# Latent attention: transposes and values one unit later, four sets of probabilities, and the exponential issued before the copy

## What is computed

```python
def probs(qb, kk):
    s = jnp.einsum("bqhd,bkhd->bhqk", qb, kk).astype(jnp.float32) * scale
    return jax.nn.softmax(s, axis=-1)
...
q_a = (_rms(acq, lp["mla_q_norm_g"]) @ lp["mla_w_q_up"]).reshape(B, N, H_A, NOPE_A + ROPE_A)
kv = (ckv_all @ lp["mla_w_kv_up"]).reshape(B, T, H_A, NOPE_A + V_A)
k_a = jnp.concatenate([kv[..., :NOPE_A],
                       jnp.broadcast_to(kr_all[:, :, None, :], (B, T, H_A, ROPE_A))], axis=-1)
o_a = _attend(jnp.concatenate([q_nope, q_rope], axis=-1), k_a, kv[..., NOPE_A:]).reshape(B, N, H_A * V_A)
```

## Time and profile before

| | us |
|---|---|
| median of 3 runs | 2758.0 |
| least and most of the runs | 2754.29, 2760.59 |
| the profiled execution | 2755.17 |
| its span, first to last instruction | 2753.3 |
| TensorE busy | 2599.3 (94% of the span) |
| GpSimd busy | 1329.9 (48%) |
| VectorE busy | 1184.5 (43%) |
| ScalarE busy | 742.3 (27%) |
| chain that ended last | PE 85%, DVE 8%, ACT 2% |

### The profile page before, as it was taken

How to read it: one execution, slowest core, us unless ns; L and a number is a source line. 1 busy time by engine, 2 the same in 40 slices (tenths; PEclk the granted TensorE clock), 3 DMA queues, 4 the chain that set the end, 5 groups by cost and what they waited for, 6 DMA issues and landing times.

```text
span 2753.3 us, 41706 instructions
## 1 busy us (share of the span) xinstructions
PE 2599.3 (94%) x17328; PEld 2405.0 (87%) x17328; DVE 1184.5 (43%) x1708; ACT 742.3 (27%) x1332; POOL 1329.9 (48%) x604
## 2 busy tenths in 40 slices
PE   4999989999999999999979999898999999999997
PEld 3879986777999899999968799668789998999997
DVE  4434255777224522232554422658752173132233
ACT  2252235215312312021123313351343023021121
POOL 2534540340565566666645255205226665666663
PEclk8999999999999999999999899999999999999999
DMA  6201215430222122222211022242102221222221
GB/s 249 69 16 60 68 58 183 170 129 1 71 75 70 62 77 74 73 77 77 74 57 47 17 74 71 93 169 85 39 27 74 77 70 62 77 70 76 77 75 56
DMA packets 62555, 215.33 MB, mean 78 GB/s; under 512 B 6688, under 2 KB 11168, under 8 KB 62112
## 3 DMA queue, kind: packets, MB, share of 16 engines
q1 hardware_dynamic: 56448, 203.97, 21.8%
q10 hardware_dynamic: 5920, 8.70, 0.9%
HBM read 208.15 MB, written 4.49 MB: 77 GB/s over the span
## 4 chain that ended last, share of the span: by engine, by line
PE 85%; DVE 8%; ACT 2%; DVEq 2%; issue 1%; DMA 1%; ACTq 1%; SPq 1%
PE big L459 22%; PE big L462 22%; PE big L463 22%; PE big L614 4%; PE last_two L645 2%; PE two L628 2%; PE last_two L541 1%; PE big L482 1%; DVE cols L1356 1%; PE two L759 1%; PE big L485 1%; PE big L486 1%; PE last_two L759 1%; DMA first_mod<-in_first 1%; DVE sq L1701 1%
## 5 line engine op out<-in xcount | busy, mean ns | idle before, releaser
L427 POOL TENSOR_TENSOR w_hi<-raw,cst 128x1024 fp32r<-128x1024 f32 x288 | 556.8, 1933 | 1295.4 <-PE big L459 1183.4
L459 PE MATMUL big<-act_hi,w_hi 128*128 128x320 f32 x2784 | 871.0, 313 | 21.6 <-ACT stage L1208 6.5
L462 PE MATMUL big<-act_lo,w_hi 128*128 128x320 f32 x2784 | 864.4, 310 | 0.0
L463 PE MATMUL big<-act_hi,w_lo 128*128 128x320 f32 x2784 | 864.1, 310 | 0.0
L430 POOL TENSOR_TENSOR w_lo<-raw,w_hi 128x1024 fp32r<-128x1024 f32 x288 | 742.4, 2578 | 41.0
L459 PEld LDWEIGHTS big<-act_hi,w_hi 128*128 128x128 f32 x2784 | 526.7, 189 | 32.5 <-issue 29.4
L462 PEld LDWEIGHTS big<-act_lo,w_hi 128*128 128x128 f32 x2784 | 526.9, 189 | 0.9
L463 PEld LDWEIGHTS big<-act_hi,w_lo 128*128 128x128 f32 x2784 | 526.3, 189 | 0.0
L459 PE MATMUL big<-u_hi,w_hi 128*128 128x320 f32 (+1 forms) x1024 | 320.6, 313 | 12.7 <-DVE cols L1793 10.8
L462 PE MATMUL big<-u_lo,w_hi 128*128 128x320 f32 (+1 forms) x1024 | 319.2, 312 | 0.0
L463 PE MATMUL big<-u_hi,w_lo 128*128 128x320 f32 (+1 forms) x1024 | 318.8, 311 | 0.0
(11 more groups left out here) (301 smaller groups left out, 3504.3 us busy)
## 6 DMA issues: line engine op xcount, KB each, us to landing
raw<-in_w SPq DMA_DIRECT2D x368, 512.0 KB, 3.5
first_mod<-in_first SPq DMA_DIRECT2D x16, 512.0 KB, 15.7
x<-in_x ACTq DMA_DIRECT2D x1, 2560.0 KB, 12.6
out_y<-x SPq DMA_DIRECT2D x8, 320.0 KB, 2.3
cst<-in_const ACTq DMA_DIRECT2D x1, 1664.0 KB, 10.9
small<-in_small ACTq DMA_DIRECT2D x2, 437.0 KB, 8.9
out_C<-c_new ACTq DMA_DIRECT2D x2, 258.0 KB
v_d<-in_past ACTq DMA_DIRECT2D x2, 256.0 KB, 3.0
```

The lines of the kernel that those rows point to most:

```text
L427: nc.gpsimd.tensor_tensor(w_hi[:, to, :], raw[:, slot, :], ones[:, 0:1].to_broadcast([P, BLK]), ALU.mult)
L459: first = mm(ps, wh, ah, start=k == 0, stop=False)
L462: mm(ps, wh, al, start=False, stop=False)
L463: last = mm(ps, wl, ah, start=False, stop=k == nk - 1)
```

## The change

The lag of transposes and values becomes a number per kind of attention: 2 for the latent attention (it was 1), 1 for the differential attention as before. In the latent attention:

- TensorE issues turn(i-2) instead of turn(i-1), and the values of the pair that ends with unit i-3.
- There are four sets of probabilities: two in `prob_a`, and `t1` and `rs` as one set each. The columns of maxima and sums go round four places instead of two, in both attentions.
- ScalarE issues exps(i+1) first and copyT(i-2) behind it. In the differential attention the exponentials stood first before and still do.
- The `w_mod` blocks stand in steps 5 to 8, the row's copy in step 9, its transposes and the keeping in step 10, one step later each.
- VectorE's outputs come one step later.

The diff, without its lines on waits that only count anew:

```diff
+MLA_LAG, DIFF_LAG = 2, 1
+COPY_FIRST = {1: False, 2: False}
...
-        neg_max, row_sum = cols[:, 12:16], cols[:, 16:20]
+        neg_max, row_sum = cols[:, 12:20], cols[:, 20:28]
...
+        LAG = {1: MLA_LAG, 2: DIFF_LAG}
+
         def prob_tile(prob, maps, i, m):
 
-            return prob[:, maps * (i % 3) + m, :] if i % 3 < 2 else (t1, rs)[m]
+            n = i % (LAG[maps] + 2)
+            if n < 2:
+                return prob[:, maps * n + m, :]
+            if maps == 1:
+                return (t1, rs)[n - 2]
+            return (t1, rs)[m] if n == 2 else sq[:, m, :]
...
-                    if p < 4 and 4 <= at < 8:
-                        if at == 4:
+                    if p < 4 and 5 <= at < 9:
+                        if at == 5:
...
-                        for k in (2 * at - 8, 2 * at - 7):
+                        for k in (2 * at - 10, 2 * at - 9):
                             mod_block(l, KD * q + k, one[1][:, 256:512])
-                    if p < 4 and at == 9:
-                        mod_turn(l, q, one[1][:, 256:512])
+                    if i >= 10 and at == 0:
+                        mod_turn(l, q - 1, one[1][:, 256:512])
...
-                for i in range(-1, n + 2):
+                lag = LAG[maps]
+                for i in range(-1, n + lag + 1):
                     if i + 1 < n:
                         scores(i + 1)
                     if beside and 0 <= i:
                         beside(i)
-                    if 0 <= i - 1 < n:
-                        turn(i - 1)
-                    if 0 <= i - 2 and (i - 2) % side == side - 1:
-                        if beside and i % 10 == 1:
-                            pe.wait_ge(mod_kept, l * MOD_CHUNKS + 3 + (i - 11) // 10)
-                        values((i - 2) // side)
+                    if 0 <= i - lag < n:
+                        turn(i - lag)
+                    j = i - lag - 1
+                    if 0 <= j and j % side == side - 1:
+                        if beside and j % 10 == 9:
+                            pe.wait_ge(mod_kept, l * MOD_CHUNKS + 3 + j // 10)
+                        values(j // side)
...
                 def exps(i):
                     h, t = units[i]
-                    if i >= 3:
-                        act.wait_ge(pT_ready, l * 60 + unit0 + i - 2)
+                    lag = LAG[maps]
+                    if i >= lag + 2:
+                        act.wait_ge(pT_ready, l * 60 + unit0 + i - lag - 1)
...
-                for i in range(-1, n + 1):
-                    if i >= 1 and maps == 1:
-                        copyT(i - 1)
+                lag = LAG[maps]
+                for i in range(-1, n + lag):
+                    if i >= lag and COPY_FIRST[maps]:
+                        copyT(i - lag)
                     if i + 1 < n:
                         exps(i + 1)
-                    if i >= 1 and maps == 2:
-                        copyT(i - 1)
+                    if i >= lag and not COPY_FIRST[maps]:
+                        copyT(i - lag)
...
-                    if i % 10 == 8:
+                    if i % 10 == 9 and i < 40:
                         keep_row(l, 2 + i // 10, one[1][:, 256:512])
```

More of the change, by code:

```diff
@@ L960, in exps @@
                         ps, b, _ = buf(use)
-                        col = 2 * (i % 2) + m
+                        col = 2 * (i % 4) + m
                         act.wait_ge(maxed, l * 80 + exp0 + maps * i + m + 1)
@@ L1361, in normalise @@
                     n = CTX if t == LATE else T
-                    c0 = 2 * (i % 2)
+                    c0 = 2 * (i % 4)
                     dve.wait_ge(exped, l * 80 + exp0 + maps * (i + 1))
@@ L1385, in attend @@
                 n = len(units)
-                for i in range(-1, n + 3):
+                lag = LAG[maps]
+                for i in range(-1, n + lag + 2):
                     if i + 1 < n:
@@ L1393, in attend @@
                         normalise(i)
-                    if i >= side + 2 and i % side == 0:
-                        outputs((i - side - 2) // side)
+                    j = i - lag - 2
+                    if j >= 0 and j % side == side - 1:
+                        outputs(j // side)
                     if beside and i >= 0:
@@ L1445, in hook @@
                 def hook(i):
-                    if i % 10 == 9 and i < 40:
-                        q = 2 + i // 10
+                    if i % 10 == 0 and 10 <= i <= 40:
+                        q = 1 + i // 10
                         keep_mod(l, q, q, one[1][:, 256:512])
```

## The result

The changed kernel takes 2781.7 us (median of 5 runs, 2777.3 to 2787.7) against 2758.0: the ratio is 1.0088, with a 95% interval of 1.0069 to 1.0107. The forecast was 2778, slower, with a range of 2765 to 2787.

What follows compares the result with a forecast made beforehand. TensorE's work plus its waits bounds the kernel. Adding +17 us for the chain and +3 for the blocks' loads to the 2758.0 us median gave 2778 us, range 2765 to 2787 (8 in 10).

Steps and rivals of the forecast that it cites:

- What bounds: Whole kernel: TensorE's work plus its waits, busy 94% of the span; the change touches only the two latent attention stages.
- the sign: Latent attention in the profile after: both stages last 116 to 119 us each, with TensorE still busy about 102.
- The chain: Latent attention: scores' start through maximum, exponential and copy to next step's turn takes about 4.0 us; TensorE's cover is 3.0 to 4.2.
- The period: Ten units of latent attention take 29.0 us against 26.5; waits of 1.3, 1.1, 0.3, 0.7 in steps 10, 12, 13, 14.
- The sum: Both latent attention stages: 7.5 us from three periods plus 1 outside them, 8.5 per layer, +17 us for two.
- The loads: Fourth block pair of each period has less time for its loads: 0.5 us on average in 8 periods, +3 us.
- The clock: Latent attention: new waits are no longer than today's 1.7 us, so the granted clock keeps 2.4 GHz.
- rival C: TensorE falls to 1.2 GHz in parts of the stage, 10 us in each of 8 periods: 2858 us; chance 2%.
- A: Faster: copies behind the early exponential are always in time, 4.8 us of waits per layer vanish: 2748 us; chance 5%.
- B: Nothing measurable: the new waits shrink to what they replace, 2753 to 2763 us; chance 5%.
- E: Slower by half: only the waits of steps 10 and 12 arise, 2.4 against 1.1 us: 2768 us; chance 15%.
- D: Slower with the loads: every fourth block pair waits a full microsecond or two: 2785 us; chance 15%.

Runs made afterwards that it cites:

- the grid: Eight versions combining lag 1 or 2, exponential or copy first, old or later block and row steps; ratios to the kernel before from 1 to 1.0088.
- the version with the lowest ratio: Against the kernel before: lag 2, copy first, blocks spread over steps 5 to 9, row's transposes in step 11, row kept before outputs; 2753.5 us, ratio 0.9977.

## Why the prediction was right

- **What bounds.** Right: the two stages grew by 24.4 us of the 26.7 between the two profiled executions, and most of what came in were waits of TensorE. The stages last 119.5 and 121.9 us, more than the 116 to 119 that I gave as the sign.
- **The chain.** Right in every link. Start of scores 12 to maximum 1.38 (forecast 1.38), to the exponential 0.92 (0.86 taken), to the copy 1.06 (1.00), to the transposes 0.42 (0.42 for the short copy). That a ready copy is held behind a waiting exponential is what the grid shows: with the exponential first there are 8.0 to 12.3 us of copy waits per layer in all four cells, with the copy first 0 to 3.5.
- **The period.** Forecast 29.0, measured 29.7, with waits of 1.42, 1.24, 0.26 and 0.78 (forecast 1.3, 1.1, 0.3 and 0.7) at the places forecast; 0.4 of the 0.7 us that are missing is the pair of blocks that a load split. Transposes of the probabilities no longer wait for VectorE, as forecast.
- **The sum: two terms, both short.** Forecast +17 for the chain and +3 for the loads, measured +24.4. The part of the loads can be taken out: from the start of a pair of blocks to the next instruction, idle time ahead of the pair included, the sixteen pairs of a layer took 16.0 and 17.2 us before and take 18.2 and 20.5 now. So the loads cost 5.5 us, and about 19 are left for the chain. The chain's waits in the period above are 3.7 us instead of 3.4: I took 0.86 for maximum to exponential, where it is 0.92, and an interval of the differential attention for exponential to copy, where it is 1.06 instead of 1.00. That is 0.3 us in each of six whole periods, 1.8 in all, and fills the gap between 17 and 19.
- **The loads.** Forecast +3, measured +5.5; this is the larger part of what was missing. TensorE's named waits for the ring account for 3.5 of it (1.0 and 3.4 us, where layer 1 had 0.9 before). The other 2 are what a pair loses beyond its idle time when a load splits it, which I hadn't priced. Per period the loads cost 0.8 us, where I took 0.5 from a span of 0 to 1.
- **The clock.** 1.00 in both stages of the profiled execution, as forecast, but this was in part luck: seven of the twelve kernels below show a fall of the clock in one stage or both, behind waits no longer than 1.7 us. A fall costs about 2 us there, not the 10 for each period that rival C priced.
- **Rivals.** A fell: the change removed the waits for probabilities and still lost; it would have needed the chain under 3.0 us. And the version nearest to A, copy first at lag 2, isn't faster either, so my price for A (-10 us) was wrong by itself: waits that are taken away come back at the next thing in line (the row, the loads, VectorE's outputs). B and E fell by the stages. D took 10 us for the loads; the 5.5 lie between it and my own 3.

My expectations for the experiments were worse than the prediction, and mostly too hopeful (only the later steps alone turned out cheaper than I expected): of the six versions from which I expected some microseconds off the kernel before, two show it beyond their interval, by 4 us at most.

## What to carry to other kernels

On an in-order engine, an instruction that waits for new work must not stand ahead of one that is ready and that somebody waits for: with a single buffer behind it (here the one tile of transposes), the whole chain from new scores to the old copy falls on the engine that bounds. A deeper pipeline didn't help here: the lag of 2 lost 4 to 10 us in the four pairs of the grid, in two of them clear of the noise. Whether a second tile for the transposes would have changed that wasn't tried. Lay the chain from start to start against the work that covers it, step by step, and look for the steps that lack their cover; and when waits are taken away, ask what is second in line before the gain is booked.

One place is left where this could be put to use. The differential attention has its exponentials first in every version, and TensorE waits for its copies in the kernel before (layer 0, 606 to 720 us):

```profile
PE two L628 <- ACT probT_d L978: 2.2, 5, 0.5
```

No run put the copy first there, so what that is worth isn't known.

## What the runs showed that I had not expected

**The clock falls in this stage in some executions.** In layer 0 of the version with copy first and old steps, TensorE waited 1.00 and 0.60 us for two loads:

```profile
426.43 0.64 PE L550 MATMUL last_two<-raw,cond 128*32 128x256 f32 x8 [1.00 <-DMA raw<-in_w]
...
427.67 0.64 PE L550 MATMUL last_two<-raw,cond 128*32 128x256 f32 x8 [0.60 <-DMA raw<-in_w]
...
431.54 2.40 PE L654 MATMUL last_two<-probT_a,v_a 128*64 128x128 f32 x20
...
437.78 1.31 PE L654 MATMUL last_two<-probT_a,v_a 128*64 128x128 f32 x20
```

The values at 431.54 last 2.40 us, the same 20 matmuls at 437.78 last 1.31. The stretches view gives the clock:

```profile
425.00:430.00 5.00, 3.25 (x27) 1.87 (x25) 1.02 (x4) 0.82 (x3) 0.00 (x0) 0.84 0.76 267
430.00:436.00 6.00, 5.69 (x32) 4.46 (x33) 0.70 (x4) 1.95 (x7) 0.00 (x0) 0.56 0.27 88
436.00:445.00 9.00, 8.82 (x61) 6.32 (x59) 6.99 (x16) 5.80 (x13) 0.00 (x0) 1.00 0.00 0
```

From 430 to 433 us alone the clock is 0.50, the lower of the two levels, 1.2 GHz, and some microseconds later it is 1.00 again. Seven of the twelve experiments show 0.96 to 0.99 in one stage or both, and seven of these eleven falls stand at the head of a stage. Here is the version with the lowest ratio, the scores of units 0 and 1 and of units 2 and 3, in layer 0 and in layer 1:

```profile
407.56 2.82 PE L623 MATMUL big<-k_a,q_a 96*128 96x320 f32 x8 [1.57 <-DVEq L1700]
410.71 4.63 PE L623 MATMUL big<-k_a,q_a 96*128 96x320 f32 x8 [0.33 <-ACT prob_a L980]
...
1758.75 2.39 PE L623 MATMUL big<-k_a,q_a 96*128 96x320 f32 x8 [1.56 <-DVEq L1700]
1761.90 2.42 PE L623 MATMUL big<-k_a,q_a 96*128 96x320 f32 x8 [0.76 <-ACT prob_a L980]
```

The same eight matmuls last 4.63 us in one layer and 2.42 in the other, behind the same wait of 1.6 us; the change has the same wait at its head and stays at 1.00. The Trainium skill (TensorE: Matmul & The Clock Gate, "Part 1: The HAM clock gate") says that idleness throttles the array to half clock. The trace agrees in the level, 0.50, and in that idle time stands ahead of these falls. But the same idle time is followed by a fall in one execution and not in the next, so why the clock falls in one and not in the other stays open. The prediction said that waits of up to 1.7 us leave the clock alone; that held for the kernel before and the change, but not here. What a fall costs can be read where the two layers differ: the same version has 0.97 in layer 0 with 108.0 us and 1.00 in layer 1 with 105.6. That is of the size of what these versions gain, so a difference of 2 or 3 us between two stages means little unless both are at 1.00.

**Where the loads cost.** A wait for the ring breaks a pair of blocks into two pieces, and what TensorE loses is more than its idle time: the pair at 453.73 and 454.55 above shows 0.18 us of idle time but takes 1.39 us instead of 1.00. Spreading the eight blocks over five steps removed every such wait in the four versions that have it.
